# Keys and values of a cross attention made in pieces between the steps of a block inversion, in a two-layer fp32 kernel

## The reference, cut to what matters

```python
D_MODEL, SEQ, N_MEM = 1024, 512, 256
h = rmsnorm(x, norm_mix)
p = h @ w_in
y_ret  = retention_mixer(p[..., :RET_PROJ], ...)
y_rwkv = rwkv7_mixer(p[..., RET_PROJ:], ...)       # wkv7_scan: a recurrence over 512 tokens
x = x + concat([y_ret, y_rwkv]) @ w_out
x = x + memory_cross_attention(rmsnorm(x, norm_xattn), rmsnorm(mem, norm_mem), w_q, w_kv, w_o)

def memory_cross_attention(h, mem_n, w_q, w_kv, w_o):
    q = (h @ w_q).reshape(B, S, 4, 256)
    k, v = jnp.split(mem_n @ w_kv, 2, axis=-1)     # 256 x 1024 each
    s = einsum('bshd,bmhd->bhsm', q, k) * 256 ** -0.5
    return einsum('bhsm,bmhd->bshd', softmax(s), v).reshape(B, S, D_MODEL) @ w_o
```

## Time and profile before

| | |
|---|---|
| Time, median of 3 runs | 1665.65 us (1665.53 to 1667.44) |
| Span of the profiled execution | 1665.8 us (no other time of that execution is given) |
| PE busy, in the span | 1598.0 us, 96% |
| DVE, ACT, POOL busy | 886.7, 655.9, 109.2 us |
| Mean granted TensorE clock | 0.997 |
| HBM | 102 GB/s over the span |

### The profile page before, as it was taken

The page is one execution under the profiler, slowest core; times in us unless marked ns, Lnnn a source line. Parts: engine busy times, 40 slices in busy tenths (PEclk is TensorE's granted clock), DMA queues, the critical chain, the costliest instruction groups (busy, mean ns, idle before and its releaser), DMA issues.

```text
span 1665.8 us, 26106 instructions
## 1 busy us (share of the span) xinstructions
PE 1598.0 (96%) x11311; PEld 1280.4 (77%) x11311; DVE 886.7 (53%) x1340; ACT 655.9 (39%) x948; POOL 109.2 (7%) x141
## 2 busy tenths in 40 slices
PE   7999997899999999999999989999899999999998
PEld 5866767877796678888888868777558788888887
DVE  6454584516445355545454654435975655555644
ACT  3215832134434245424141254456783422221210
POOL 1300105000000000000000020012300000000000
PEclk9999999999999999999999999999999999999999
DMA  6612220005342243645444442221003233333222
GB/s 213 182 51 63 67 85 4 5 28 167 111 140 89 85 152 124 225 127 179 152 157 170 158 129 83 61 76 67 1 14 114 70 87 97 101 102 101 92 83 79
DMA packets 150692, 170.30 MB, mean 102 GB/s; under 512 B 14296, under 2 KB 111202, under 8 KB 150194
## 3 DMA queue, kind: packets, MB, share of 16 engines
q1 hardware_dynamic: 142424, 156.82, 29.9%
q10 hardware_dynamic: 8154, 11.81, 2.6%
HBM read 164.12 MB, written 6.33 MB: 102 GB/s over the span
## 4 chain that ended last, share of the span: by engine, by line
PE 84%; DVE 7%; ACT 4%; issue 2%; DMA 1%; POOL 1%; ACTq 0%; SPq 0%; DVEq 0%; POOLq 0%
PE ps L389 67%; PE ps L1255 4%; PE ps L1435 2%; DVE weights_low L412 1%; DMA sb_arena<-sb_arena 1%; PE ps L2690 1%; PE ps L1661 1%; PE ps L2447 1%; PE ps L2435 1%; PE ps L2467 1%; PE ps L895 1%; DVE sb_hT L2543 1%; PE ps L907 1%; ACT weights_high L409 1%; ACT sb_arena L672 1%
## 5 line engine op out<-in xcount | busy, mean ns | idle before, releaser
L389 PE MATMUL ps<-left_high,weights_high 128*128 128x512 f32 (+1 forms) x1016 | 403.4, 397 | 9.2 <-DVE left_low L694 3.6
L412 DVE TENSOR_TENSOR weights_low<-sb_weights_raw,weights_high 128x2048 fp32r<-128x2048 f32 (+1 forms) x118 | 265.3, 2248 | 258.3 <-ACT weights_high L409 258.2
L389 PE MATMUL ps<-left_high,weights_low 128*128 128x512 f32 (+1 forms) x1016 | 395.8, 390 | 0.0
L389 PE MATMUL ps<-left_low,weights_high 128*128 128x512 f32 (+1 forms) x1016 | 395.7, 390 | 0.0
L409 ACT CAST weights_high<-sb_weights_raw 128x2048 fp32r<-128x2048 f32 (+1 forms) x118 | 221.4, 1876 | 323.9 <-PE ps L389 282.6
L389 PEld LDWEIGHTS ps<-left_high,weights_high 128*128 128x128 f32 (+1 forms) x1016 | 190.1, 187 | 64.8 <-issue 13.7
L389 PEld LDWEIGHTS ps<-left_high,weights_low 128*128 128x128 f32 (+1 forms) x1016 | 190.1, 187 | 40.9
L389 PEld LDWEIGHTS ps<-left_low,weights_high 128*128 128x128 f32 (+1 forms) x1016 | 190.2, 187 | 40.0 <-issue 1.7
L389 PE MATMUL ps<-weights_high,hidden_high 128*128 128x512 f32 x432 | 169.0, 391 | 0.0
L389 PE MATMUL ps<-weights_high,hidden_low 128*128 128x512 f32 x432 | 168.2, 389 | 0.0
L389 PE MATMUL ps<-weights_low,hidden_high 128*128 128x512 f32 x432 | 168.1, 389 | 0.0
(11 more groups left out here) (418 smaller groups left out, 2111.0 us busy)
## 6 DMA issues: line engine op xcount, KB each, us to landing
sb_weights_raw<-in_w_in SPq DMA_DIRECT2D x25, 1024.0 KB, 5.3
sb_yT<-in_ada_w SPq DMA_DIRECT2D x24, 1024.0 KB, 5.2
sb_weights_raw<-in_ffn_w_up SPq DMA_DIRECT2D x44, 512.0 KB, 5.1
sb_weights_raw<-in_mlp_w_up SPq DMA_DIRECT2D x16, 1024.0 KB, 6.3
sb_weights_raw<-in_mlp_w_down SPq DMA_DIRECT2D x16, 1024.0 KB, 7.8
sb_weights_raw<-in_ffn_w_down SPq DMA_DIRECT2D x10, 1024.0 KB, 5.0
sb_weights_raw<-in_xattn_w_kv SPq DMA_DIRECT2D x8, 1024.0 KB, 5.2
sb_weights_raw<-in_w_out SPq DMA_DIRECT2D x6, 1024.0 KB, 5.0
```

Source lines behind the costliest of these rows:

```text
L389: last = nc.tensor.matmul(o, lhsT, rhs, start=b["first"] and i == 0, stop=b["last"] and i == len(pairs) - 1)
L412: nc.vector.tensor_tensor(l[:, 0:n], raw[:, 0:n], h[:, 0:n].bitcast(F32), ALU.subtract).then_inc(w_low, 1)
```

## The change

The projection to keys and values leaves `w_qkv`. `w_q` stays there with four chunks. The eight chunks of `kv` stand in the stream between `w_in` and `w_out`, and their blocks have four units each (6 matmuls of 256 columns for K, 3 of 512 for V). The units are taken in the inversion (4 in the first twelve product blocks, 52 between the steps) and in the grams (8). They use banks 6 and 7; the inversion and the grams use the other six. The inversion becomes one chain of 20 steps, in which PE makes block Y of step i, block X of step i-1 and then two or three units. The norm of the memory moves to the front; its split parts lie over X, which is loaded again after the grams. Keys and values are stored to DRAM as they come and loaded again at the start of `w_q`.

```diff
-            return 2 if b["n"] == S else 1
+            return b.get("units") or (2 if b["n"] == S else 1)
...
@@ load_params_act
+            a.eng.dma_start(MEMR, A["mem"].rearrange("a (t p) d -> p (a t) d", p=P)).then_inc(mem_moved, 16)
@@ front1_pe
-            fill(dense, 8)
+            fill(dense, 2)
+            memory_turn_pe(pe)
+            fill(dense, 6)
             fill(dense, 5)
+            pe.wait_ge(norm_low, pe.count(norm_low))
@@ front1_act
-            fill(dense, 4)
+            fill(dense, 3)
+            memory_squares_act(a)
+            fill(dense, 1)
...
-            fill(dense, 18)
+            fill(dense, 5)
+            memory_high_act(a)
+            fill(dense, 13)
@@ front1_dve
-            fill(dense, 10)
+            fill(dense, 6)
+            memory_rows_dve(v)
+            fill(dense, 4)
             for n in range(4):
                 rotate_dve(v, n)
                 fill(dense, 2)
+                if n == 1:
+                    memory_low_dve(v)
@@ invert_pe
+        GRAM_ORDER = [(0, 0), (1, 0), (0, 1), (1, 1), (2, 0), (2, 1), (0, 2), (1, 2), (0, 3), (1, 3), (2, 2), (2, 3)]
+        INV_FILL = [3, 2] * 10 + [2]
+        N_INV = 5 * NPAIR
+            def y_sum(i):
+                lv, u = 1 + i // NPAIR, i % NPAIR
+                pe.wait_ge(inv_masked, i + 1)
+                pe.wait_ge(inv_ready, max(i + 1, 3 if i == 1 else 0))
+                if i == 0:
+                    pe.wait_ge(inv_xt_kept, 3)
+                if i >= 2:
+                    pe.wait_ge(inv_y_kept, i - 1)
+                chunk_products(i % 2, of_pairs(MASKED[lv % 2]), of_pairs(XM), u, crossed=True).then_inc(inv_y, 1)
+            def x_sum(i):
+                pe.wait_ge(inv_y_kept, i + 1)
...
+                chunk_products(4 + i % 2, of_pairs(YM), of_pairs(XT), u,
+                               beside=(2 + i % 2, of_pairs(XT), of_pairs(YM)) if lv < 5 else None).then_inc(inv_x, 1)
...
+            for i in range(N_INV + 1):
+                if i < N_INV:
+                    y_sum(i)
+                if i:
+                    x_sum(i - 1)
+                fill(dense, INV_FILL[i])
@@ invert_act
+            for i in range(N_INV + 1):
+                if i < N_INV:
+                    a.wait_ge(inv_y, i + 1)
+                    nc.scalar.copy(YM[:, i % NPAIR], bank_pair(i % 2)).then_inc(inv_y_kept, 1)
+                fill(dense, INV_FILL[i])
@@ grams_pe (N_GRAM_BANKS = 6 in place of 8; the same fill in grams_act and grams_dve)
+                if n % 3 == 2:
+                    fill(dense, 1)
@@ grams_act, at its end
+            fill(dense, units(kv) + 1)
+            for i in range(2):
+                a.eng.dma_start(X[:, 2 * i:2 * i + 2, :], A["x"][0, 256 * i:256 * i + 256, :].rearrange(
+                    "(t p) d -> p t d", p=P)).then_inc(x_loaded[i], 16)
@@ the products
-        MEMH = rounded_at("memory_high", arena_base, 18432, KT, M)
+        MEMH = rounded_at("memory_high", X_base, 0, KT, M)
+        KV_OUT = hT2[:, 6:8, :]
+        def kv_part(n, at, w, closes):
+            def evac(a, src, free, value):
+                if n >= 2 and at == 0:
+                    a.wait_ge(first_loaded if n % 2 else mem_moved, 16 * (n // 2) + (32 if n % 2 else 16))
+                nc.scalar.copy(KV_OUT[:, n % 2, at:at + w], src).then_inc(free, 1)
+                if closes:
+                    a.wait_ge(free, value)
+                    a.eng.dma_start(kv_dram[n], KV_OUT[:, n % 2, :]).then_inc(
+                        first_loaded if n % 2 else mem_moved, 16)
+            return evac
+        def load_kv_act(a):
+            a.wait_ge(acc_done, w_out[1]["blocks"][-1]["acc"])
+            a.eng.dma_start(KX..., kv_dram[0:4]...)          # one load for K, two for V
...
-        STREAM = lay_stream([w_in, w_out, w_qkv, w_o, ...
+        STREAM = lay_stream([w_in, kv, w_out, w_q, w_o, ...
@@ w_out_dve
+            for i in range(2):
+                v.wait_ge(x_loaded[i], 32)
@@ w_q_pe, w_q_act, w_q_dve: the products of w_q alone
+            load_kv_act(a)
+            fill(evac_steps(a, "act", w_q), 1 + units(w_q))
```

More of the change, by code:

```diff
@@ L259, in pairs, with by_token @@
                 return out_
-            return dict(pairs=pairs, m=m, n=n, first=True, last=True, owner=owner, evac=evac, other=other)
-        def by_token(c0, w_, lhs, owner, evac, nk=KT, k0=0, first=True, last=True):
+            return dict(pairs=pairs, m=m, n=n, first=True, last=True, owner=owner, evac=evac, other=other,
+                        units=units)
+        def by_token(c0, w_, lhs, owner, evac, nk=KT, k0=0, first=True, last=True, units=None):
             def pairs(wh, wl):
@@ L270, in pairs @@
                 return out_
-            return dict(pairs=pairs, m=P, n=w_, first=first, last=last, owner=owner, evac=evac, other=None)
+            return dict(pairs=pairs, m=P, n=w_, first=first, last=last, owner=owner, evac=evac, other=None,
+                        units=units)
         def kview(w):
@@ L427, in evac_steps @@
                 for b in ch["blocks"]:
-                    if units_of(b) == 2:
+                    for _ in range(units_of(b) - 1):
                         yield
@@ L1272, in invert_pe @@
             for n in (-2, -1):
                 kept_by_act(pe, w_in, n)
[L1274 to L1294, removed]
@@ L1299, in invert_act @@
             a.eng.dma_start(GUP1[0:32], A["rwkv_g_up"][0, P:P + 32]).then_inc(front_loaded, 16)
-            a.skip(inv_gram, 2 * NPAIR)
             for u in range(NPAIR):
[L1302 to L1307, removed]
+                a.wait_ge(inv_gram, GRAM_AT[2, u])
+                nc.scalar.copy(MT[:, u], bank_pair(2 + u % 2)).then_inc(inv_kept, 1)
+                if u % 2:
+                    fill(dense, 2)
+            for i in range(N_INV + 1):
[3 more added lines that the diff above has]
+                fill(dense, INV_FILL[i])
         def masks_pool(g):
@@ L3032, in w_out_dve @@
             rwkv_out_dve(v, dense)
+            for i in range(2):
+                v.wait_ge(x_loaded[i], 32)
             fill(dense, units(w_out) - 17)
             closing_norm_dve(v, dense, w_out, NORM_2)
-        def memory_part(k):
-            return ps[:, 4 + k // 2, (k % 2) * M:(k % 2) * M + M]
-        def w_qkv_pe(pe):
-            dense = product_steps(pe, w_qkv, 4)
-            fill(dense, 8)
-            for k in range(KT):
-                for t in range(2):
-                    if k == 0:
-                        pe.wait_ge(rows_normed, pe.count(rows_normed))
-                    last = nc.tensor.transpose(memory_part(k)[:, t * P:(t + 1) * P], HS[:, t, k * P:(k + 1) * P], ident)
-                if k % 2:
-                    last.then_inc(turned, 1)
-            fill(dense, 8)
-            pe.wait_ge(norm_low, pe.count(norm_low))
-            fill(dense, 1 + units(w_qkv))
@@ L3053, in w_qkv_act @@
-        def w_qkv_act(a):
-            dense = evac_steps(a, "act", w_qkv)
-            fill(dense, 2)
-            a.wait_ge(mem_loaded, a.count(mem_loaded, 16))
-            for t in range(2):
-                squares_act(a, NORM_3, t)
-            fill(dense, 6)
-            for k in range(0, KT, 2):
-                a.wait_ge(turned, a.count(turned))
-                for i in range(2):
-                    last = nc.scalar.activation(MEMH[:, k + i, :], memory_part(k + i), ACT.Copy,
-                                                scale=col("norm_mem", k + i))
-                last.then_inc(norm_high, 1)
-            fill(dense, 1 + units(w_qkv))
@@ L3068, in w_qkv_dve, with w_q_pe @@
-        def w_qkv_dve(v):
-            dense = evac_steps(v, "dve", w_qkv)
-            fill(dense, 4)
-            for t in range(2):
-                rows_dve(v, NORM_3, t)
-            fill(dense, 4)
-            for k in range(0, KT, 2):
-                v.wait_ge(norm_high, v.count(norm_high))
-                for i in range(2):
-                    last = nc.vector.scalar_tensor_tensor(out=MEML[:, k + i, :], in0=memory_part(k + i),
-                                                          scalar=col("norm_mem", k + i),
-                                                          in1=MEMH[:, k + i, :].bitcast(F32),
-                                                          op0=ALU.mult, op1=ALU.subtract)
-            last.then_inc(norm_low, 1)
-            fill(dense, 1 + units(w_qkv))
+        def w_q_pe(pe):
+            fill(product_steps(pe, w_q, 4), 1 + units(w_q))
```

198 lines of the change are left out of this document (146 added, 52 removed).

## The result

The changed kernel takes 1669.13 us (median of 20 runs, 1667.0 to 1671.31) against 1666.89 us for the kernel before in the same comparison (20 runs). The ratio is 1.0015, 95% interval 1.0009 to 1.0021: slower, by 2.2 us. Forecast was 6.65 us faster, with a range of its own of 1653 to 1665. The time lies inside the wide range (1648 to 1673), and the difference is less than the 0.2% that the prediction counts as no change; but the interval excludes a gain, and the direction is wrong. Most of the work behaved as forecast, so the question is narrow: in the two profiled spans, 1.5 us more stand where 6.65 us less were forecast.

What follows compares the result with a forecast made beforehand. PE, busy 96% of the span, bounds the kernel, with instruction waits in the inversion to fill. From 1665.8 us, -46.55 + 2.7 + 28.0 + 9.2 = -6.65 gives 1659.1 us; own range 1653 to 1665, 8-in-10 range 1648 to 1673.

Steps and rivals of the forecast that it cites:

- w_qkv: Projection stage before the attention: K and V work and the memory's turning taken away, -46.55 us.
- Front, to the retention: Before the retention: eight subtractions on DVE delay its start, partly offset by less contention; +2.7 us, from +1.0 to +5.
- D: Retention's start: the front's wait of about 3.5 us lowers the clock, costing 1.7 us (1660.8); within the forecast's 0.58.
- Inversion: Inversion: small blocks at the array's pace plus dense units and mode changes, 96.0 us against 67.96; +28.0 us.
- Grams to scan: Grams through the scan's start: eight dense V units and a longer stage end, 32.5 against 23.33 us; +9.2 us.
- the prediction's signs of being wrong: Inversion issue waits over 5 us, dense groups under 0.1 us extra, or PE waiting on ACT copies or DVE adds.
- The issue waits: PE's waits without releaser in the inversion, read as waiting for instructions; near 1 us expected in place of 12.3.
- Rival A: Inversion: issue waits stay, so dense work is added at 45.7 us in place of 28.0; 1676.9 us, chance 0.15.
- Rival C: Splits of weights on ACT and DVE delay PE's copies or adds by 7.2 us; 1666.3 us, chance 0.12.
- Rival B: Mode changes among short matmuls are free and the front absorbs its 2.7 us; 1647.7 us, chance 0.15.
- the 0.28: Inversion and grams: price in us per dense group for changing PE between quarters and whole array, 0.23 plus 0.05.
- The half clock at 252.3: Inversion of the kernel before: half clock from 252.3 to 255.7 after a wait, expected gone.

Runs made afterwards that it cites:

- low4: Changed kernel with the memory's eight low-part subtractions behind the fourth rotary turn, not between second and third; 1662.99 us, ratio 0.9967 to the kernel before.
- both: Changed kernel with the memory's subtractions behind the fourth turn and X loaded again by SP instead of ACT; 1661.92 us, ratio 0.9961 to the kernel before.
- early: Kernel 'both' with the grams' dense fills one phase earlier (n % 3 == 0 instead of 2); 1659.62 us, ratio 0.9958 to the kernel before.
- before_x: Kernel before with only the reload of X from the change, issued by ACT after its last gram eviction; 1668.5 us, ratio 1.0006 to the kernel before.
- last: Changed kernel with all 52 dense units behind the last inversion step, none between steps; 1678.9 us, ratio 1.006 to the kernel before.
- both_grp: Kernel 'both' with the 50 units between steps taken five at a time behind every second step, 10 groups fewer; 1662.14 us, ratio 0.9963 to the kernel before.
- both_fine: Kernel 'both' with one unit per step taken between blocks Y and X, 19 groups more; 1668.85 us, ratio 1.0003 to the kernel before.
- early_act: Kernel 'low4' with the grams' fills at n % 3 == 0, X still loaded by ACT; 1661.67 us, ratio 0.9957 to the kernel before.
- xsp: Changed kernel with the two loads of X issued by SP instead of ACT; 1666.62 us, ratio 0.999 to the kernel before.

## Why the prediction was wrong, point by point

The sum by its own steps, each from the chain or the stretches of the two profiled executions (stage starts of before: 88.35, 238.38, 306.34, 329.67, 370.06, 423.72, 514.92; of after: 92.11, 244.47, 340.78, 373.82, 416.69, 470.34, 514.83):

| Step | forecast, us | measured, us |
|---|---|---|
| w_qkv | -46.55 | 44.49 - 91.20 = -46.71 |
| Front, to the retention | +2.7 | +3.76 |
| Retention to inversion | 0 (1.7 in D) | 152.36 - 150.03 = +2.33 |
| Inversion | +28.0 | 96.31 - 67.96 = +28.35 |
| Grams to scan | +9.2 | 33.04 - 23.33 = +9.71 |
| Scan | 0 | 42.87 - 40.39 = +2.48 |
| w_out part | 0 | 53.65 - 53.66 = 0 |
| From the attention to the end | 0 | 1152.47 - 1150.88 = +1.6 |
| Sum | -6.65 | +1.5 |

**The step that failed is the clock: the sum held the half clock behind the new waits at nothing, and it cost 4.8 us.** Behind the front's wait it was a rival's detail (D, 1.7 us) and no term of the sum; at the scan it wasn't named at all. After the front PE waits 4.6 us and runs 6.8 us at half clock: from the retention to the inversion it takes 152.36 us, where the kernel before takes 150.03 and 'low4', at full clock, 238.72 - 88.67 = 150.05. That is +2.33. The prediction did work out the gap ahead of the scan, 2.2 us from the last block; it was 371.14 to 373.82, 2.7 us from the last matmul's start. The slow stretch there cost 2.48 us in the changed kernel and 2.75 between 'both' and 'early'. Knowing that a wait of 2.5 us before had 3.4 us of half clock behind it, I should have asked of each wait of that size that the change makes, not only of the front's. None of the prediction's signs of being wrong looked at the clock, and none of them came up.

**The second failure is a size: the front's +2.7 came out at +3.76.** That is within its own bounds of +1 to +5, and the mechanism is as forecast. The chain: the eight subtractions cost 3.14 us, and the third turn's first operation fell from 1.71 to 0.61, as forecast; that is 2.04, and with 0.23 from an earlier row SP's exchange starts 2.27 us later. But the exchange itself took 6.34 us in place of 4.96, another 1.38, and 0.1 us came ahead of the retention's first matmul. The forecast had named the late exchange in its range and given it hardly anything in the sum. The longer transfer stands in all four executions in which the subtractions come ahead of the exchange (6.34 to 6.53 us); in 'low4', where they come behind it, it is 4.94 us. Which other transfer it meets wasn't tested and stays open: the load of weights behind it is issued 1.23 us later in both kernels, so that distance isn't it. Delay and half clock together make the front +6.1 us, about what 'low4' gives back.

Front with its half clock 3.4 us over forecast, scan 2.5, the remainder after the attention 1.6, inversion and grams 0.9, less 0.2: that is the difference of 8.2 us. The 1.6 us contain stretches of half clock near 988 us (0.57 in the row above, 1.00 in the kernel before) and near 1302 us, where the kernel before has none. The second execution of the changed kernel has the first of them and not the other, the second of the kernel before the other and not the first; 'before_x' has one at 989 and 'early' one at 978, while 'both' has none there and 6.8 us of half clock near 965 instead. I can't tie the 1.6 us to the change, and they stay open.

**What was right.** The issue waits are PE waiting for its instructions: they went from 12.3 to 1.1 us by filling, came back as 12.5 us without it ('last'), and end at one distance behind the packets. Rival A is out; a fixed price of dispatch would have kept them, and the Trainium skill's "mostly hidden" ("Runtime: NRT & Kernel Launch", "Instruction fetch mechanics") doesn't hold for this stage, where 12.3 of 67.96 us were such waits. The inversion was forecast at 96.0 and is 96.3 and 96.0. Rival C is out: PE waits neither for ACT's copies nor for DVE's adds in the chain of steps. Rival B is out as well: groups cost 0.23 us (ten fewer, 'both_grp') to 0.38 us (19 more, 'both_fine') each, around the 0.28 assumed. Two more readings lie near them. In the grams of the changed kernel three product blocks take 2.94 us and a dense group 0.89; three blocks at 0.943 and a unit at 0.68 would take 3.51, so a group costs 0.32 us there, and eight of them make up most of the 0.5 us over forecast. 'last' has 20 groups fewer and PE is busy only 95.15 - 92.50 = 2.65 us less, 0.13 a group, but with 3.4 us of half clock in it. So the 0.28 is an average that came out right and not a price that is known; with 0.38 for 23 groups the inversion would have been forecast 2.3 us longer, and its near hit (96.0 against 96.3) may in part be luck. The Trainium skill's rule that a change of tiling mode drains the array ("TensorEngine Tiling (Array Packing)", "Key Properties") is in line with a price above nothing in each of the four; that draining is what costs it, no run here shows.

The half clock at 252.3 is gone, as expected: the inversion's row has 1.00 where it had 0.97. But the kernel before had it in one of its two profiled executions only, so this is no merit of the change that the runs establish.

## What to carry to other kernels

Where an engine of small instructions waits with no releaser in the profile, count its records per instruction packet; long instructions laid between them recover that time, a few per group, and each group has a price of its own to be measured. When work is moved into "idle" time of an engine, look whether the next thing in its program starts a transfer or releases the bound engine: here 3.1 us of subtractions one transfer too early cost 6 us with the half clock behind them, and behind the transfer they cost 0.3. Ask the clock column about every place where TensorE gets a new wait and price the half clock with it, and try to let the last filler stand ahead of some of the stage's own work, not at its end.

## What the runs showed of the hardware that I had not expected

The half clock lasted as long (6.8 us) after PE's wait of 2.3 us as after that of 4.6 us, and in 'both' after one of 1.2 us. Its price isn't half its length: of 6.8 us 2.3 to 2.75 us were lost. PE has gaps in these places (5.09 us busy of 6.75, 5.78 of 6.78).

A wait of 1.2 us was followed by full clock in 'before_x' and 'early_act' and by half clock in 'both', 'both_grp', 'both_fine' and 'xsp', with the same matmuls behind it.

The last transfer of the same exchange of halves took 4.9 to 5.0 us in nine executions, with the exchange's first issue between 71.5 and 72.5 us, and 6.34 to 6.53 us in four, with that issue between 73.8 and 74.4 us (both executions of the changed kernel, 'xsp', 'last').
